# Expert stage of a two-block model: a plain-fp32 gather with the first expert apart, and the order of the last weight loads

## The chip, the cores and the metric

One core of one Trainium2 chip runs the whole program in one launch. The metric is the device time in microseconds (us). Three runs of the kernel before are shown; their median is the number that the change is measured against.

## The reference

The model is two blocks, all in fp32: a hybrid of a state-space mixer, a gated recurrence and a feed-forward layer over 528 tokens, then attention, a second recurrence and an expert layer over 512 tokens. The change touches only the expert layer, which is the last thing before the final normalisation:

```python
def expert_choice_ffn(h, w_router, w_gate, w_up, w_down):
    b, s, d = h.shape                      # 1, 512, 1024
    cap = EC_CAPACITY * s // N_EXPERTS     # 64 tokens for each of 16 experts
    affinity = jax.nn.softmax((h @ w_router).astype(jnp.float32), axis=-1)
    top_val, top_idx = lax.top_k(affinity.transpose(0, 2, 1), cap)
    xe = jax.vmap(lambda hb, ib: hb[ib])(h, top_idx)
    act = jax.nn.silu(jnp.einsum('becd,edf->becf', xe, w_gate)) * jnp.einsum('becd,edf->becf', xe, w_up)
    ye = jnp.einsum('becf,efd->becd', act, w_down) * top_val[..., None].astype(h.dtype)
    return jax.vmap(lambda yb, ib: jnp.zeros((s, d), yb.dtype).at[ib.reshape(-1)].add(yb.reshape(-1, d)))(ye, top_idx)

    # the end of the second block
    x = x + expert_choice_ffn(rms_norm(x, norm_ffn_g[l]), w_router[l], w_exp_gate[l], w_exp_up[l], w_exp_down[l])
    return rms_norm(x, norm_final_g)
```

Each expert picks its 64 tokens of 512. Gate and up weights are 1024 x 2048, down weights 2048 x 1024, so the 16 experts read 403 MB.

## The kernel before, in words

`two_blocks` calls the stages one after the other. The last is `expert_ffn` (names in the trace begin with `moe_`). All engines run their own instruction streams, written out by hand and tied by semaphores.

**Chunks and the ring.** An expert's 2048 hidden columns are cut into 4 chunks of 512, so there are 64 chunks, n = 0 to 63, with e = n // 4 the expert and c = n % 4 its chunk. Each chunk has three weight pieces of 2 MB: part 0 is gate, 1 is up, 2 is down. They pass through `ring`, a buffer of 7 slots. The list `items` gives the order of the loads: gate and up of chunk n, then down of chunk n - 1. The SyncE engine issues one DMA for each item (L3485); from the eighth item on it first waits until the item 7 places back is used: for gate and up that is `hidden_made`, for down it is `out_made`.

**Routing.** TensorE makes the logits (L3494), VectorE the affinities (L3726 to L3733). `turn_tokens` (L3503) transposes the raw rows `xg` to token-major form. ScalarE scales them into `z_high` in fp32r (`split_high`, L3647), and VectorE writes the rest that fp32r cut off into `z_low` (`split_low`, L3740). VectorE finds each expert's 64 largest affinities in 8 rounds of 8 (L3747 and L3748), and in seven of these rounds a `split_low` stands behind the two search instructions. A scan gives each chosen token its place (L3752), and `one_hot(b)` (L3762) makes the selection matrix `hot` for a batch of 4 experts, 256 columns.

**Gather.** `gather(b, v)` (L3532) multiplies token rows by `hot`: 2 blocks of 128 features, 4 blocks of 128 tokens, and two passes (low and high), 16 fp32r matmuls in all with 256 columns each; `take` (L3663) copies the result to `xe`, which lies in `xg`. Batch 0 runs its four gathers before the first chunk; those of batch b + 1 stand one behind the last chunk of each expert of batch b.

**A chunk on TensorE.** `hidden(n, half)` (L3550) is 8 fp32 matmuls of 64 x 512 a half, gate and up in two halves of the array. Between its halves stands `turn(n - 1)` (L3564), the transposes of the activation of the chunk before, which ScalarE copies to `act_t` (L3677). Then comes `output(n - 1)` (L3578), 8 matmuls with down weights. On ScalarE `silu` (L3670) and on VectorE `product` (L3779) make the activation. For each expert, `turn_scatter` (L3589) makes the matrix that puts rows back, and `combine` (L3603), from the chunk after the next expert's first on, multiplies it with `ye` (copied at L3804); VectorE adds to `acc` (L3787). The loop over n has one more pass than chunks, for the last turn and output. Then come the last four combines, the final sums of squares (L3629, L3640), the scale (L3705, L3707), eight scalings (L3811) and eight stores (L3488).

In the profile a plain fp32 matmul stands as two records and an fp32r one as one, each with its own weight load; transposes have one record.

## Time and profile before

| | before |
|---|---|
| runs | 2951.44, 2952.47, 2947.84 us |
| median of the three | 2951.44 us |
| profiled execution, span from first to last instruction | 2951.6 us |
| profiled execution, its own time | given only as that span |
| TensorE matmul busy | 2675.1 us (91%) |
| TensorE weight loads busy | 1940.4 us (66%) |
| VectorE busy | 1261.7 us (43%) |
| ScalarE busy | 800.0 us (27%) |
| mean granted TensorE clock | 0.960 of full |
| largest shares of the chain that ended last | DMA 21%, TensorE 11%, VectorE 1% |
| HBM read, written | 568.84 MB, 38.99 MB |

The span is what one profiled execution took on the core; the runs are separate executions. Busy shares are means over stages with different limits: the expert stage begins at 1967 us and lasts a third of the span. The chain of waits is followed back from the last instruction, at each step to what released it. A granted clock of 1.00 is 2.4 GHz and 0.50 is 1.2 GHz.

### The profile page before, as it was taken

How to read it: one execution, taken by the hardware profiler on the slowest of the kernel's cores; microseconds unless marked ns; L12 is line 12 of the kernel's file. 1: busy time of each engine (PE TensorE's matmuls, PEld its weight loads, DVE VectorE, ACT ScalarE, POOL GpSimd, SP SyncE). 2: the span in 40 equal slices, each digit the busy share in tenths (PEclk: the TensorE clock that was granted, in tenths of full speed). 3: DMA queues.
4: the chain of work that ended last, by engine and by line, in shares of the span. 5: the costliest groups of instructions: out<-in, count | busy, mean ns of one | idle time of the engine just before them, and what ended most of it. 6: DMA issues, size and time to landing. Idle time of an engine off the chain costs nothing. (4 is left out here: it accounts for less than half of the span.)

```text
span 2951.6 us, 44568 instructions
## 1 busy us (share of the span) xinstructions
PE 2675.1 (91%) x18822; PEld 1940.4 (66%) x18822; DVE 1261.7 (43%) x2123; ACT 800.0 (27%) x1304; POOL 112.8 (4%) x90
## 2 busy tenths in 40 slices
PE   8997789799999998999889999879989899989887
PEld 8996677699999998778668888654333333333222
DVE  7764666444566632666363335751111111111112
ACT  3220454432434321543253332531000000000001
POOL 0000021000000000000002221000000000000000
PEclk9998899899999999999989999989999999999999
DMA  5447331455322233334420000548999999999996
GB/s 161 130 129 120 108 123 61 149 164 159 114 90 86 78 123 129 114 129 154 161 77 1 2 1 34 176 179 363 430 430 431 430 431 430 431 431 431 431 430 258
DMA packets 144437, 613.09 MB, mean 208 GB/s; under 512 B 37808, under 2 KB 57392, under 8 KB 119216
## 3 DMA queue, kind: packets, MB, share of 16 engines
q1 hardware_dynamic: 120576, 574.13, 50.7%
q10 hardware_dynamic: 23664, 36.11, 3.5%
q8 instruction: 151, 2.47, 0.3%
q14 instruction: 46, 0.38, 0.0%
HBM read 568.84 MB, written 38.99 MB: 206 GB/s over the span
## 5 line engine op out<-in xcount | busy, mean ns | idle before, releaser
L3550 PE MATMUL moe_bank<-moe_ring,xg 128*64 128x512 f32 x2048 | 494.1, 626 | 90.6 <-DMA moe_ring<-in_w_exp_up 89.3
L3550 PEld LDWEIGHTS moe_bank<-moe_ring,xg 128*64 128x64 f32 x2048 | 156.0, 142 | 370.9 <-issue 362.1
L3779 DVE TENSOR_TENSOR moe_sg<-moe_sg,moe_bank 64x512 f32<-64x512 f32 x64 | 44.1, 690 | 584.7 <-ACT moe_sg L3670 584.7
L3578 PE MATMUL moe_bank<-moe_ring,moe_act_t 128*64 128x512 f32 x1024 | 230.6, 592 | 0.5 <-ACT moe_act_t L3677 0.5
L66 PE MATMUL ffn_prod<-ffn_x_low,ffn_w_high 128*128 128x264 f32 x704 | 200.7, 285 | 5.9 <-PEq L142 5.9
L66 PE MATMUL in_bank<-x_low,in_w_high 128*128 128x264 f32 x640 | 187.3, 293 | 17.9 <-DVE in_w_low L982 9.2
L68 PE MATMUL ffn_prod<-ffn_x_high,ffn_w_high 128*128 128x264 f32 x704 | 200.9, 285 | 0.0
L67 PE MATMUL ffn_prod<-ffn_x_high,ffn_w_low 128*128 128x264 f32 x704 | 199.9, 284 | 0.0
L68 PE MATMUL in_bank<-x_high,in_w_high 128*128 128x264 f32 x640 | 184.6, 288 | 0.0
L67 PE MATMUL in_bank<-x_high,in_w_low 128*128 128x264 f32 x640 | 184.3, 288 | 0.0
L3578 PEld LDWEIGHTS moe_bank<-moe_ring,moe_act_t 128*64 128x64 f32 x1024 | 73.3, 137 | 146.3 <-issue 145.7
L3677 ACT COPY moe_act_t<-moe_bank 128x256 f32<-128x256 f32 x64 | 23.8, 372 | 515.7 <-PE moe_bank L3564 515.7
L66 PE MATMUL front_bank<-front_x_low,front_w_high 128*128 128x512 f32 x368 | 147.9, 402 | 11.8 <-DVE front_w_low L2505 11.7
L3787 DVE TENSOR_TENSOR acc<-acc,moe_bank 128x512 f32<-128x512 f32 x128 | 82.2, 684 | 174.2 <-PE moe_bank L3603 174.2
L67 PE MATMUL front_bank<-front_x_high,front_w_low 128*128 128x512 f32 x368 | 144.3, 392 | 0.0
L68 PE MATMUL front_bank<-front_x_high,front_w_high 128*128 128x512 f32 x368 | 144.1, 392 | 0.0
L66 PEld LDWEIGHTS ffn_prod<-ffn_x_low,ffn_w_high 128*128 128x128 f32 x704 | 133.1, 189 | 6.1 <-issue 6.1
L66 PEld LDWEIGHTS in_bank<-x_low,in_w_high 128*128 128x128 f32 x640 | 123.2, 192 | 19.6 <-issue 9.6
L67 PEld LDWEIGHTS ffn_prod<-ffn_x_high,ffn_w_low 128*128 128x128 f32 x704 | 133.2, 189 | 0.0
L68 PEld LDWEIGHTS ffn_prod<-ffn_x_high,ffn_w_high 128*128 128x128 f32 x704 | 133.0, 189 | 0.0
L67 PEld LDWEIGHTS in_bank<-x_high,in_w_low 128*128 128x128 f32 x640 | 123.8, 193 | 0.4 <-issue 0.2
L68 PEld LDWEIGHTS in_bank<-x_high,in_w_high 128*128 128x128 f32 x640 | 123.5, 193 | 0.0
(549 smaller groups left out, 5696.8 us busy)
## 6 DMA issues: line engine op xcount, KB each, us to landing
moe_ring<-in_w_exp_gate SPq DMA_DIRECT2D x64, 2048.0 KB, 27.7
moe_ring<-in_w_exp_up SPq DMA_DIRECT2D x64, 2048.0 KB, 21.3
moe_ring<-in_w_exp_down SPq DMA_DIRECT2D x64, 2048.0 KB, 25.9
front_w<-in_w_in SPq DMA_DIRECT2D x50, 512.0 KB, 3.6
ffn_w<-in_w_up SPq DMA_DIRECT2D x44, 512.0 KB, 4.4
in_w<-in_w_in SPq DMA_DIRECT2D x40, 512.0 KB, 4.1
ffn_w<-in_w_down SPq DMA_DIRECT2D x16, 704.0 KB, 4.0
p<-front_out ACTq DMA_DIRECT2D x35, 256.0 KB, 2.0
```

The source lines that it names most:

```text
L66: nc.tensor.matmul(to, w_high, x_low, start=start, stop=False)
L67: nc.tensor.matmul(to, w_low, x_high, start=False, stop=False)
L68: return nc.tensor.matmul(to, w_high, x_high, start=False, stop=stop)
L3550: last = nc.tensor.matmul(bank[64 * g:64 * g + 64, s], xe[:, (e // BATCH) % 2, k, at:at + CAPACITY], ring[:, slot_of(n, g), k * HALF:(k + ...
L3578: last = nc.tensor.matmul(bank[64 * h:64 * h + 64, 3 + e % 2], act_t[:, s, j], ring[:, slot, at:at + HALF], start=(c == 0 and j == 0), sto ...
L3677: nc.scalar.copy(act_t[:, s].rearrange("p j n -> p (j n)"), bank[:, 2, s * FT * CAPACITY:(s + 1) * FT * CAPACITY]).then_inc(act_t_ready, 1)
L3779: nc.vector.tensor_tensor(sg[0:CAPACITY, s], sg[0:CAPACITY, s], bank[64:64 + CAPACITY, s], ALU.mult).then_inc(act_ready, 1)
L3787: nc.vector.tensor_tensor(acc[:, FT * h + q], acc[:, FT * h + q], bank[:, part_bank(e, q) + h], ALU.add).then_inc(part_added, 1)
```

## The change

It has three parts.

1. `z_tok` and `hot` are plain fp32. There is no `z_low`: ScalarE's copies (`take_tokens`) are the whole of the token rows, the eight `split_low` on VectorE are gone, and a gather has one matmul in fp32 where it had two in fp32r.
2. Batch 0 is gathered in parts. `gather_first` gathers the first expert alone before the first chunk, with 32 matmuls of 64 columns into bank 4, and `take_first` copies them. The other three experts follow in four gathers of 8 matmuls with 192 columns, one behind each chunk of expert 0, through banks 5 and 6. `hidden` waits for the first copy at n = 0 and for all of batch 0 at n = 4. Batches 1 to 3 keep their places, with 8 matmuls of 256 columns.
3. The last seven items are gate and up of chunks 62 and 63 and then down of 61, 62 and 63. TensorE's last steps are written out in that order.

```diff
-        z_tok = sb("z_tok", [P, 2, TT, D_MODEL], F32R)
-        z_high, z_low = z_tok[:, 0], z_tok[:, 1]
-        hot_r = sb("hot", [P, 2, TT, BATCH, CAPACITY], F32R)
-        hot = hot_r[:].bitcast(F32)
+        z_tok = sb("z_tok", [P, TT, D_MODEL])
+        hot = sb("hot", [P, 2, TT, BATCH, CAPACITY])
...
-        for n in range(CHUNKS_ALL + 1):
-            if n < CHUNKS_ALL:
-                items += [(n, 0), (n, 1)]
+        for n in range(LAST):
+            items += [(n, 0), (n, 1)]
             if n >= 1:
                 items += [(n - 1, 2)]
+        items += [(n, part) for n in (LAST, LAST + 1) for part in range(2)] + [(n, 2) for n in (LAST - 1, LAST, LAST + 1)]
...
+                def gather_first():
+                    pe.wait_ge(hot_ready, 1)
+                    for k in range(KT):
+                        for t in range(TT):
+                            last = nc.tensor.matmul(bank[:, 4, k * CAPACITY:(k + 1) * CAPACITY], z_tok[:, t, k * P:(k + 1) * P],
+                                                    hot[:, 0, t, 0], start=(t == 0), stop=(t == TT - 1))
+                    last.then_inc(xe_made, 1)
+
                 def gather(b, v):
-                    to = 4 + v if b == 0 else 7
-                    if v == 0:
+                    if b == 0:
+                        to, first = 5 + v % 2, 1
+                        if v >= 2:
+                            pe.wait_ge(xe_ready, v)
+                    else:
+                        to, first = 7, 0
                         pe.wait_ge(hot_ready, b + 1)
-                    if b >= 1:
                         pe.wait_ge(scatter_ready, BATCH * (b - 1) + v + 1)
+                    width = (BATCH - first) * CAPACITY
                     for j in range(2):
                         k = 2 * v + j
                         for t in range(TT):
-                            for part in (z_low, z_high):
-                                last = nc.tensor.matmul(bank[:, to, j * WIDE:(j + 1) * WIDE], part[:, t, k * P:(k + 1) * P],
-                                                        hot_r[:, b % 2, t].rearrange("p e s -> p (e s)"),
-                                                        start=(t == 0 and part is z_low),
-                                                        stop=(t == TT - 1 and part is z_high))
+                            last = nc.tensor.matmul(bank[:, to, j * width:(j + 1) * width], z_tok[:, t, k * P:(k + 1) * P],
+                                                    hot[:, b % 2, t, first:].rearrange("p e s -> p (e s)"),
+                                                    start=(t == 0), stop=(t == TT - 1))
...
-                for v in range(BATCH):
-                    gather(0, v)
-                pe.wait_ge(xe_ready, BATCH)
-                for n in range(CHUNKS_ALL + 1):
+                gather_first()
+                for n in range(LAST + 1):
                     e, c = n // FC, n % FC
-                    if n < CHUNKS_ALL:
-                        hidden(n, 0)
+                    hidden(n, 0)
                     if n >= 1:
                         turn(n - 1)
-                    if n < CHUNKS_ALL:
-                        hidden(n, 1)
-                    if n >= 1:
+                    hidden(n, 1)
+                    if 1 <= n < LAST:
                         output(n - 1)
-                    if n < CHUNKS_ALL and c == 2:
+                    if e == 0:
+                        gather(0, c)
+                    if c == 2:
                         turn_scatter(e)
-                    if n < CHUNKS_ALL and c == 3 and e // BATCH + 1 < BATCHES:
+                    if c == 3 and e // BATCH + 1 < BATCHES:
                         gather(e // BATCH + 1, e % BATCH)
                     if n >= FC + 1:
                         combine((n - FC - 1) // FC, (n - FC - 1) % FC)
+                for half in range(2):
+                    hidden(LAST + 1, half)
+                combine(EXPERTS - 2, FC - 2)
+                output(LAST - 1)
+                turn(LAST)
+                output(LAST)
+                combine(EXPERTS - 2, FC - 1)
+                turn(LAST + 1)
+                output(LAST + 1)
...
                 for r in range(CAPACITY // 8):
                     step(nc.vector.max(best[:], left))
                     step(nc.vector.match_replace(left, best[:], left, -1.0))
-                    if r >= 1:
-                        split_low(r)
```

The order on TensorE from the last place transposes to the end of chunk 1, before (`moe_hot` by `moe_z_tok` is a gather, `moe_ring` by `xg` is hidden, `moe_ring` by `moe_act_t` is output):

```order
L3517 MATMUL moe_bank<-ident,moe_sg 128x16 x4
L3532 MATMUL moe_bank<-moe_hot,moe_z_tok 128x256 x64
L3550 MATMUL moe_bank<-moe_ring,xg 64x512 x24
L3564 MATMUL moe_bank<-ident,moe_sg 128x64 x4
L3550 MATMUL moe_bank<-moe_ring,xg 64x512 x8
L3578 MATMUL moe_bank<-moe_ring,moe_act_t 64x512 x8
```

The same place now:

```order
L3519 MATMUL moe_bank<-ident,moe_sg 128x16 x4
L3528 MATMUL moe_bank<-moe_hot,moe_z_tok 128x64 x32
L3564 MATMUL moe_bank<-moe_ring,xg 64x512 x16
L3545 MATMUL moe_bank<-moe_hot,moe_z_tok 128x192 x8
L3564 MATMUL moe_bank<-moe_ring,xg 64x512 x8
L3578 MATMUL moe_bank<-ident,moe_sg 128x64 x4
L3564 MATMUL moe_bank<-moe_ring,xg 64x512 x8
L3592 MATMUL moe_bank<-moe_ring,moe_act_t 64x512 x8
L3545 MATMUL moe_bank<-moe_hot,moe_z_tok 128x192 x8
```

The 64 wide gather matmuls became 32 narrow ones; hidden(0) is now followed by a gather, and hidden(1) with its turn and output(0) by the next.

The order on TensorE at the end, from hidden(62) on, before:

```order
L3550 MATMUL moe_bank<-moe_ring,xg 64x512 x8
L3578 MATMUL moe_bank<-moe_ring,moe_act_t 64x512 x8
L3589 MATMUL moe_bank<-ident,moe_hot_aff 128x128 x4
L3603 MATMUL moe_bank<-moe_scatter,moe_ye 128x512 x2
L3550 MATMUL moe_bank<-moe_ring,xg 64x512 x8
L3564 MATMUL moe_bank<-ident,moe_sg 128x64 x4
L3550 MATMUL moe_bank<-moe_ring,xg 64x512 x8
L3578 MATMUL moe_bank<-moe_ring,moe_act_t 64x512 x8
L3603 MATMUL moe_bank<-moe_scatter,moe_ye 128x512 x2
L3564 MATMUL moe_bank<-ident,moe_sg 128x64 x4
L3578 MATMUL moe_bank<-moe_ring,moe_act_t 64x512 x8
L3603 MATMUL moe_bank<-moe_scatter,moe_ye 128x512 x8
```

The same place now, from the second half of hidden(62):

```order
L3564 MATMUL moe_bank<-moe_ring,xg 64x512 x8
L3603 MATMUL moe_bank<-ident,moe_hot_aff 128x128 x4
L3617 MATMUL moe_bank<-moe_scatter,moe_ye 128x512 x2
L3564 MATMUL moe_bank<-moe_ring,xg 64x512 x16
L3617 MATMUL moe_bank<-moe_scatter,moe_ye 128x512 x2
L3592 MATMUL moe_bank<-moe_ring,moe_act_t 64x512 x8
L3578 MATMUL moe_bank<-ident,moe_sg 128x64 x4
L3592 MATMUL moe_bank<-moe_ring,moe_act_t 64x512 x8
L3617 MATMUL moe_bank<-moe_scatter,moe_ye 128x512 x2
L3578 MATMUL moe_bank<-ident,moe_sg 128x64 x4
L3592 MATMUL moe_bank<-moe_ring,moe_act_t 64x512 x8
L3617 MATMUL moe_bank<-moe_scatter,moe_ye 128x512 x6
```

The output of chunk 61 moved behind hidden(63), turn(62) moved out of hidden(63) to stand right before its output, and the last combine of expert 14 stands ahead of the last turn instead of behind the last output.

## Rows read from the trace of the kernel before

**Rows 1.** Chain of waits: start us, us, engine, what, at the stage's middle and end.

```profile
2588.57 3.65 PE moe_bank L3550 x16
...
2617.71 3.65 PE moe_bank L3550 x16
...
2910.97 3.65 PE moe_bank L3550 x16
...
2918.60 3.43 PE moe_bank L3578 x16
2922.03 1.06 PE moe_bank L3603 x4
2923.79 3.65 PE moe_bank L3578 x16
2927.44 1.08 PE moe_bank L3603 x4
```

**Rows 2.** Windows: length, busy us of each engine, granted clock, DMA share, GB/s.

```profile
2004.00:2013.00 9.00, 8.28 (x44) 3.92 (x44) 0.00 (x0) 1.89 (x3) 0.00 (x0) 1.00 0.00 0
2013.50:2014.00 0.50, 0.50 (x4) 0.17 (x2) 0.40 (x1) 0.07 (x1) 0.00 (x0) 1.00 0.96 197
```

**Rows 3.** Timeline from the search to the second release of the ring: start us, us.

```profile
1973.74 0.68 DVE L3747 MAX8 moe_best<-moe_sg 16x8 f32<-16x512 f32 x1
...
1975.23 0.68 DVE L3747 MAX8 moe_best<-moe_sg 16x8 f32<-16x512 f32 x1
...
1977.40 0.67 DVE L3747 MAX8 moe_best<-moe_sg 16x8 f32<-16x512 f32 x1
...
1993.69 1.22 DVE L3762 TENSOR_TENSOR moe_hot<-slots,moe_place_tok 128x1024 fp32r<-128x1024 f32 x1
...
1995.06 10.07 PE L3532 MATMUL moe_bank<-moe_hot,moe_z_tok 128*128 128x256 f32 x64 [1.74 <-DVE moe_hot L3762]
...
2005.85 10.52 PE L3550 MATMUL moe_bank<-moe_ring,xg 128*64 128x512 f32 x48 [0.72 <-ACT xg L3663]
...
2012.97 0.33 SPq L3485 DMA_DIRECT2D moe_ring<-in_w_exp_down  x1
...
2020.38 0.33 SPq L3485 DMA_DIRECT2D moe_ring<-in_w_exp_up  x1
```

**Rows 4.** Windows at two changes of the granted clock.

```profile
1969.00:1970.00 1.00, 1.00 (x8) 1.00 (x7) 0.00 (x0) 0.98 (x2) 0.00 (x0) 0.64 0.54 229
1995.00:2000.00 5.00, 4.94 (x23) 4.97 (x24) 0.64 (x1) 0.59 (x1) 0.00 (x0) 0.50 1.04 441
2000.00:2003.00 3.00, 3.00 (x27) 3.00 (x27) 0.00 (x0) 0.59 (x1) 0.00 (x0) 1.00 0.96 410
```

**Rows 5.** Timeline, 128x128 fp32 weights at half and full clock, and under one column.

```profile
1545.39 0.55 PEld L2942 LDWEIGHTS rw_bank<-rw_sm,rw_a_first 128*128 128x128 f32 x2
1545.82 0.55 PEld L2943 LDWEIGHTS rw_bank<-rw_z,rw_sm 128*128 128x128 f32 x2
...
1805.23 0.30 PEld L2942 LDWEIGHTS rw_bank<-rw_sm,rw_a_first 128*128 128x128 f32 x2
1805.45 0.30 PEld L2943 LDWEIGHTS rw_bank<-rw_z,rw_sm 128*128 128x128 f32 x2
...
1965.64 1.05 PE L3274 MATMUL merge_bank<-merge_one,merge_sq_sum 128*128 128x1 f32 x8
```

**Rows 6.** Timeline near the end: a half-clock group, the last turn, the waiting add.

```profile
2896.38 5.35 PE L3550 MATMUL moe_bank<-moe_ring,xg 128*64 128x512 f32 x16 [2.49 <-DMA moe_ring<-in_w_exp_up]
...
2922.92 0.40 PE L3564 MATMUL moe_bank<-ident,moe_sg 64*128 64x64 f32 x4
...
2928.55 1.28 DVE L3787 TENSOR_TENSOR acc<-acc,moe_bank 128x512 f32<-128x512 f32 x2 [0.37 <-PE moe_bank L3603]
```

**Rows 7.** Timeline, a gather of batch 1 between chunks.

```profile
2046.12 2.18 PE L3532 MATMUL moe_bank<-moe_hot,moe_z_tok 128*128 128x256 f32 x16
```

**Rows 8.** Line L3485, the ring's loads from issue to landing.

```profile
DMA to landing us min/median/max: 7.6/25.8/34.4
```

More of the change, by code:

```diff
@@ L3386, in expert_ffn @@
     CHUNKS_ALL = EXPERTS * FC
+    LAST = CHUNKS_ALL - 2
     WIDE = BATCH * CAPACITY
@@ L3428, in expert_ffn @@
         z_turned = sem("z_turned")
-        z_high_ready = sem("z_high_ready")
         z_tok_ready = sem("z_tok_ready")
@@ L3452, in expert_ffn, with gathers_through @@
         stored = sem("stored")
+        def gathers_through(b):
+            return 1 + BATCH * (b + 1)
         def part_bank(e, q):
@@ L3540, in hidden @@
                     if half == 0:
-                        if n % (BATCH * FC) == 0:
-                            pe.wait_ge(xe_ready, BATCH * (e // BATCH + 1))
+                        if n == 0:
+                            pe.wait_ge(xe_ready, 1)
+                        elif n == FC or n % (BATCH * FC) == 0:
+                            pe.wait_ge(xe_ready, gathers_through(e // BATCH))
                         if n >= 2:
@@ L3654, in _ @@
                 act.wait_ge(scale_ready, 1)
-                split_high(0)
+                take_tokens(0)
                 act.wait_ge(route, MOE_LOGITS)
@@ L3658, in _, with take_first @@
                 for n in range(1, 2 * TT):
-                    split_high(n)
+                    take_tokens(n)
+                def take_first():
+                    act.wait_ge(xe_made, 1)
+                    nc.scalar.copy(xe[:, 0, :, 0:CAPACITY], bank[:, 4].rearrange("p (k n) -> p k n", k=KT)).then_inc(xe_ready, 1)
                 def take(b, v):
-                    act.wait_ge(xe_made, BATCH * b + v + 1)
-                    nc.scalar.copy(xe[:, b % 2, 2 * v:2 * v + 2], bank[:, 4 + v if b == 0 else 7].rearrange(
+                    to, first = (5 + v % 2, CAPACITY) if b == 0 else (7, 0)
+                    act.wait_ge(xe_made, gathers_through(b - 1) + v + 1)
+                    nc.scalar.copy(xe[:, b % 2, 2 * v:2 * v + 2, first:], bank[:, to, 0:2 * (WIDE - first)].rearrange(
                         "p (k n) -> p k n", k=2)).then_inc(xe_ready, 1)
@@ L3684, in turned_scatter @@
                     nc.scalar.copy(scatter[:, e % 2], bank[:, 7]).then_inc(scatter_ready, 1)
-                for v in range(BATCH):
-                    take(0, v)
+                take_first()
                 for n in range(CHUNKS_ALL + 1):
@@ L3693, in _ @@
                         silu(n)
+                    if e == 0:
+                        take(0, c)
                     if n < CHUNKS_ALL and c == 2:
@@ L3759, in one_hot @@
                     if b >= 2:
-                        dve.wait_ge(xe_made, BATCH * (b - 1))
+                        dve.wait_ge(xe_made, gathers_through(b - 2))
                     grid = [P, TT, BATCH, CAPACITY]
-                    nc.vector.tensor_tensor(hot_r[:, b % 2], slots[:].unsqueeze(1).unsqueeze(1).broadcast_to(grid),
+                    nc.vector.tensor_tensor(hot[:, b % 2], slots[:].unsqueeze(1).unsqueeze(1).broadcast_to(grid),
                                             place_tok[:, :, BATCH * b:BATCH * b + BATCH].unsqueeze(3).broadcast_to(grid),
```

15 lines of the change are left out of this document (4 added, 11 removed).

## The prediction

> **What bounds the kernel now.** I read the chain of waits first. From the middle of the expert stage to its end it alternates between TensorE and the ring load of an up weight: chunk after chunk TensorE finishes early and waits for DMA. Equal places in it lie 29.14 us apart for two chunks, 2588.57 and 2617.71 [rows 1], so a chunk of three 2 MB loads takes 14.57 us and one load 4.86 us. The end of the kernel is therefore the start of an unbroken run of loads, plus 4.86 us each, plus a tail after the last.
>
> Then the windows around the start of the stage. The ring takes seven loads, and the eighth waits for the first chunk's hidden matmuls. Between 2004 and 2013 us the DMA engines carry nothing (share 0.00); from 2013.5 on they are busy [rows 2]. So the start of the first expert is the one place where an earlier TensorE brings the whole train of 185 remaining loads forward, one for one. The instruction that decides it is the SyncE issue at 2012.97 [rows 3].
>
> At the end, the chain leaves DMA at 2910.97, when the last up weights have landed. Two down pieces follow, so the last load lands about 2 x 4.86 later, at L = 2920.7. The last output matmuls start at 2923.79 and end at 2927.44 [rows 1], 6.7 us after L: the end is held by TensorE's work, not by the last transfer alone. Everything behind 2927.44 (24.2 us to the end of the 2951.6 us span) is the same in both kernels but for one add.
>
> **Term 1, the places chain on VectorE.** A round of the top-64 search without the split takes 1.49 us (1973.74 to 1975.23), one with it 2.17 us (1975.23 to 1977.40) [rows 3]. The eight splits go; the first lay beside other work, seven lay in rounds: 7 x 0.66 = 4.6 us. The one-hot at 1993.69 starts and the gather at 1995.06 [rows 3] moves to 1990.4. The ScalarE copies stay where they are and are done long before.
>
> **Term 2, the first gather.** Before: 64 matmuls of 256 columns in fp32r, one record each, 10.07 us [rows 3], the first 4.9 us at a granted clock of 0.50 (1.2 GHz), the rest at 1.00 (2.4 GHz) [rows 4]. Now: 32 matmuls with 64 columns in plain fp32. Plain fp32 matmuls show as two records each, so 64 records again, and each carries a 128x128 weight load. In the stage before, such weight loads come in pairs 0.43 us apart at half clock (1545.39, 1545.82) and 0.22 us apart at full clock (1805.23, 1805.45), so 0.215 and 0.11 us a record; eight records with a single column take 1.05 us, again 0.11 apart [rows 5]. A narrow matmul thus costs its weight load: four times fewer columns save nothing. 64 records cost 13.8 us at half clock, 7.0 us at full clock, 9.5 us if the clock rises 4.9 us in as before (23 records at 0.215, 41 at 0.11).
>
> Which? The clock fell to 0.5 inside 1969 to 1970 although TensorE ran without a break (PE 1.00, PEld 1.00): what it had just run were narrow matmuls, 1 column [rows 5], then transposes [rows 4]. It rose at 2000 after five microseconds of 256-column matmuls. The new gather is of the narrow kind, so I take half clock for the whole of it: 1990.4 + 13.8, plus 0.2 for the last record, is 2004.4. The evacuation stays 0.7 us (2005.13 to 2005.85) [rows 3], so hidden(0) starts at 2005.1 instead of 2005.85: 0.75 us gained.
>
> But hidden(0) then begins at half clock, and before it ran at full clock. A group of 16 that began just before a half-clock stretch took 5.35 instead of 3.65 us [rows 6]. I estimate that the clock rises 4.6 us into hidden(0), about as long as the 4.9 us after 1995.06; this loses half of that, 2.3 us (bounds 0 and 7.1, the whole of hidden(0), which took 7.1 from 2005.85 to 2012.97 [rows 3]). Term 2 with term 1: the eighth load is issued 2.3 - 0.75 = **1.55 us later** than before (bounds -7 and +6.4).
>
> The Trainium skill, page "TensorE: Matmul & The Clock Gate", section "LDWEIGHTS (loading the stationary operand)", prices a weight load at its columns over 1.2 GHz whatever the clock. By it, an estimate, 64 loads of 128 columns would be 6.8 us even at half clock. The pairs at half clock contradict it, with 0.215 us a record.
>
> **Term 3, feeding the ring in the first expert.** The other three experts of the batch are now gathered between the chunks, four times 8 matmuls of 192 columns: 16 records. The 128-column records of rows 5 cost 0.11 us at full clock; in proportion 192 columns are 0.16 and 256 columns 0.21, so 2.6 us a gather. Batches 1 to 3 gather 256 columns: 16 x 0.21 = 3.4 us instead of 2.1 (2.18 us with the last one's drain) [rows 7]; the 1.3 us more, twelve times, lie in the TensorE idle time of a chunk: 14.57 less 7.4 + 3.4 + 1.1 = 2.7 us, and slots are freed several loads ahead. If that cover failed it would cost 12 x 1.3 = 16 us, but landings take 25.8 us from issue at the median [rows 8], five loads ahead.
>
> Right after T, the end of hidden(0), there is no such lead. Two loads go out at T; the next two after a gather and hidden(1) with its turn, 2.6 + 7.4 = 10.0 us on (7.4 from the issue at 2012.97 to that at 2020.38 [rows 3]). The shortest landing is 7.6 us after issue [rows 8], so the third lands at T + 17.6 instead of T + 7.6 + 2 x 4.86 = T + 17.3: 0.3 us lost. Adding output 3.4, gather 2.6 and hidden 7.4 a chunk, 0.6 for turning the scatter and 3.4 for the batch-1 gather, hidden(4) ends at T + 54.2; the 12th load lands at T + 61.8 instead of 61.4: 0.4 more. **Sum 0.7 us** (bounds 0, and 3 if each gather takes 0.5 us longer). From then on TensorE needs 12 us a chunk against 14.57.
>
> **Term 4, the end.** The last up weights now land three loads before the last, at L - 14.6. From there TensorE owes hidden(63) 7.1, combine 1.06, output(61) 3.4 (2918.60 to 2922.03), turn and its copy 0.87 (2922.92 [rows 6] to 2923.79), output(62) 3.4, combine 1.06, turn 0.87, output(63) 3.65 = 21.4 us: L + 6.8 [rows 1]. Before it was L + 6.7. The loads were permuted, and the work behind them with them. The add that waited 0.37 us for its combine after the last output [rows 6] is already made: -0.35. Against that, the slack before hidden(63) shrinks from 2.0 us to 0.6 (hidden(62) at L - 24.3, then 7.4, 0.5 to 0.6 for the scatter turn and 1.1; before, output(61) lay there too, and the next load was 4.86 us further off), so the 1.7 us half-clock loss of rows 6, which was hidden, would show with 1.1; I take half of it. **Sum +0.2 us** (bounds -3.3, the last output waiting for its load alone, and +1.5).
>
> **Sum.** 1.55 + 0.7 + 0.2 = +2.5 us. The span of 2951.6 becomes 2954.1; the median of the three runs, 2951.44, is 0.2 below the span, so **2953.9 us**. That is 0.08%; a measurement of this kernel can tell about 0.2%, 5.9 us, from no change.
>
> **Rivals.** (a) *The clock rises during the gather as before.* Gather 9.5 us, hidden(0) at full clock from 2000.8: 5.05 us earlier; with terms 3 and 4 -4.1 us, **2947.3**. For it: it rose 4.9 us into the old gather, and TensorE has no gaps now either. Against it: the fall at 1969.3 under narrow matmuls.
> (b) *Weight loads do not slow with the clock.* 64 x 0.11 = 7.0 us: hidden(0) at 1998.3, 7.5 us earlier, less 2.3 for its own half clock; with 3 and 4 -4.3 us, **2947.1**, and up to 2945 if the clock rises sooner. Against it: the half-clock pairs of rows 5. That is also what the page's rule would give here.
> (c) *The end loses its TensorE queue*: output(63) waits only for its load: 3.3 us less in term 4 instead of +0.2, **2950.4**. Against it: the 21.4 us counted above.
> (d) *Slower: the clock stays low through all of hidden(0).* 7.1 us instead of 2.3, the ring then fed late with 2.7 instead of 0.7, and the 1.1 us at the end in full: 4.8 + 2.0 + 0.6 more, **2961.3**. It decides once the SyncE issue comes more than about 5 us later than 2012.97. For it: TensorE pauses 0.7 us between gather and hidden(0). Against it: wide matmuls raised the clock within 5 us.
> (e) *The change does not do what it says*, DMA still stopping for as long, is near my forecast: the stop gets longer, not shorter.
>
> **Chances.** Forecast 0.60; (a) 0.18; (b) 0.07; (c) 0.05; (d) 0.10. The forecast's own range is 2951 to 2957.5, from the bounds of terms 2 to 4. The whole range reaches to (a) and (b) below and part of the way to (d): 2946 to 2958. Faster than 2945.5: the lower edges of (a) and (b), 0.10. Slower than 2957.3: (d) and the upper edge of the forecast, 0.16. Within 0.2%: 0.74.
>
> **What would show it.** The one-hot at about 1989, the gather at 1990.4 and 13 to 14 us long with a granted clock of 0.50 all through; the SyncE issue of the eighth load at about 2014.5; gathers of 2.6 us between the first chunks; hardly any DMA pause after 2016; the last output matmuls ending about 6.8 us after the last landing. The forecast is wrong if the gather runs at 1.00 after some microseconds or its records come 0.11 us apart at half clock, if loads pause again in the first expert, or if the last output starts on its load.

## The result, and the profile after

The kernel with the change took 2956.32 us (median of 17 runs, 2953.18 to 2962.97), the kernel before 2951.17 us (17 runs, 2945.82 to 2955.27): a ratio of the means of 1.0021 with a 95% interval of 1.0015 to 1.0027. It is slower by 4.4 to 8.0 us: clear of no change, but only 0.2%. Measured again beside the last experiments it was 2956.53 against 2952.01, 1.0017 (1.0008 to 1.0026). The medians lie 5.15 us apart, and 4.5 us the second time; the forecast was 2953.9 us, 2.5 us above before, with a range of 2946 to 2958.

The page of the profiled execution (its own time 2954.39 us):

```profile
span 2952.5 us, 44691 instructions
...
PE 2698.3 (91%) x18886; PEld 1959.4 (66%) x18886; DVE 1256.3 (43%) x2115; ACT 799.4 (27%) x1305; POOL 112.6 (4%) x90
...
DMA 18%; PE 14%; DVE 1%; ACT 0%; issue 0%; DVEq 0%; ACTq 0%
...
L3564 PE MATMUL moe_bank<-moe_ring,xg 128*64 128x512 f32 x2048 | 486.7, 619 | 72.3 <-DMA moe_ring<-in_w_exp_up 71.7
```

The hidden matmuls (now L3564) still wait for up weights and for little else. What changed lies at the two ends of that train of loads. Its start, as the timeline of the kernel after (start us, us, engine, line):

```profile
1970.47 0.68 DVE L3767 MAX8 moe_best<-moe_sg 16x8 f32<-16x512 f32 x1
...
1971.96 0.68 DVE L3767 MAX8 moe_best<-moe_sg 16x8 f32<-16x512 f32 x1
...
1985.80 1.22 DVE L3780 TENSOR_TENSOR moe_hot<-slots,moe_place_tok 128x1024 f32<-128x1024 f32 x1
...
1987.17 13.89 PE L3528 MATMUL moe_bank<-moe_hot,moe_z_tok 128*128 128x64 f32 x64 [1.74 <-DVE moe_hot L3780]
...
2001.73 9.07 PE L3564 MATMUL moe_bank<-moe_ring,xg 128*64 128x512 f32 x32 [0.68 <-ACT xg L3685]
...
2010.84 0.33 SPq L3487 DMA_DIRECT2D moe_ring<-in_w_exp_down  x1
...
2021.20 0.33 SPq L3487 DMA_DIRECT2D moe_ring<-in_w_exp_up  x1
...
2024.52 2.87 PE L3545 MATMUL moe_bank<-moe_hot,moe_z_tok 128*128 128x192 f32 x16
```

And its windows (length, busy us of the engines, granted clock, DMA share, GB/s):

```profile
1976.00:1977.00 1.00, 0.00 (x0) 0.00 (x0) 0.96 (x2) 0.00 (x0) 0.00 (x0) 0.50 0.88 377
1988.00:2000.00 12.00, 12.00 (x59) 12.00 (x58) 0.00 (x0) 0.00 (x0) 0.00 (x0) 0.50 1.01 429
2001.50:2005.50 4.00, 3.77 (x10) 1.23 (x12) 0.00 (x0) 1.46 (x2) 0.00 (x0) 0.50 0.00 0
2006.00:2010.00 4.00, 4.00 (x22) 1.32 (x20) 0.00 (x0) 0.00 (x0) 0.00 (x0) 1.00 0.00 0
...
2930.00:2934.00 4.00, 4.00 (x12) 1.40 (x12) 2.26 (x4) 1.42 (x3) 0.00 (x0) 0.60 0.00 0
```

Against [rows 3]: every search round is 1.49 us, and the gather takes 13.89 us in place of 10.07. TensorE was busy for all of 1988 to 2000, yet the granted clock was 0.50 (1.2 GHz), and it stayed there through the first 4 us of hidden(0); before, it rose in the gather [rows 4].

In this execution the stages ahead, which are the same code, were 3 us shorter (in the 13 profiles the expert stage begins anywhere from 1963.4 to 1970.8 us), so all that follows counts from the stage's first ring load (1967.16 before, 1964.23 after). "Eighth issue" is the SyncE issue that hidden(0) releases (2012.97 in [rows 3], 2010.84 here); the column "hidden(0)" runs from its first matmul to that issue. A load lands with the last of its 16 completions; "last landing" is that of the 192nd weight load, 2920.52 before and 2920.69 after. All pieces are in us, from one profiled execution each, so a whole stage can lie some 3 us off what the medians say; the experiments are already in the table.

| kernel | first load to gather | gather | hidden(0) | first load to eighth issue | eighth issue to last landing | last landing to end | whole stage |
|---|---|---|---|---|---|---|---|
| before | 27.90 | 10.07 | 7.12 | 45.81 | 907.55 | 31.09 | 984.45 |
| the change | 22.94 | 13.89 | 9.11 | 46.61 | 909.85 | 31.82 | 988.28 |
| the change, again | 22.94 | 13.89 | 9.08 | 46.58 | 910.32 | 31.86 | 988.76 |
| only the end of the change | 27.48 | 9.61 | 7.12 | 44.93 | 907.69 | 32.85 | 985.47 |
| only plain fp32 | 22.94 | 16.56 | 7.11 | 47.34 | 907.85 | 31.12 | 986.31 |
| change, old end | 22.94 | 13.89 | 9.17 | 46.68 | 911.08 | 31.11 | 988.87 |
| two experts first | 23.55 | 9.33 | 7.12 | 40.72 | 909.70 | 30.91 | 981.33 |
| 128 columns, 64 used | 23.35 | 10.25 | 7.13 | 41.41 | 912.20 | 33.03 | 986.64 |
| unused wide matmuls | 22.78 | 7.25 | 7.12 | 37.83 | 910.63 | 31.86 | 980.32 |
| late gathers | 23.37 | 13.89 | 9.44 | 47.37 | 910.30 | 31.84 | 989.51 |
| two experts, late | 23.42 | 9.46 | 7.12 | 40.72 | 907.48 | 30.85 | 979.05 |
| two experts, late, again | 22.94 | 10.10 | 7.11 | 40.87 | 907.65 | 30.96 | 979.48 |
| the same with unused matmuls | 22.94 | 8.98 | 7.12 | 39.76 | 907.72 | 33.03 | 980.51 |

The change loses 3.8 us in the stage (4.3 the second time): 0.8 before the eighth issue, 2.3 (2.8) between it and the last landing, and 0.7 (0.8) behind that. The medians are 1.3 us (0.2 us) further apart than that; no piece accounts for it.

The end, timeline of the kernel after:

```profile
2906.25 7.09 PE L3564 MATMUL moe_bank<-moe_ring,xg 128*64 128x512 f32 x32 [0.41 <-DMA moe_ring<-in_w_exp_up]
...
2924.24 3.65 PE L3592 MATMUL moe_bank<-moe_ring,moe_act_t 128*64 128x512 f32 x16 [0.46 <-ACT moe_act_t L3704]
2929.97 4.56 PE L3617 MATMUL moe_bank<-moe_scatter,moe_ye 64*128 64x512 f32 x12 [2.08 <-DVE acc L3805]
```

The last output ends 7.2 us after the last landing (6.9 before, [rows 1]). TensorE then stands idle for 2.08 us until the combines of the last expert. In the kernel before, a combine lay there first and only 1.48 us were idle:

```profile
2929.98 1.99 PE L3603 MATMUL moe_bank<-moe_scatter,moe_ye 64*128 64x512 f32 x8 [1.48 <-DVE acc L3787]
```

And the combines after the change run into a stretch at half clock: the clock was 0.60 on average over 2930 to 2934.

### The profile page after: what moved, and what is told of

Its sections match the earlier page's. It is cut to its first block and busy times, and to the rows that moved or that the text cites. A ratio compares the mean times of both kernels' runs of the same rounds, so it can differ in the third digit from the quotient of the medians.

```text
span 2952.5 us, 44691 instructions
## 1 busy us (share of the span) xinstructions
PE 2698.3 (91%) x18886; PEld 1959.4 (66%) x18886; DVE 1256.3 (43%) x2115; ACT 799.4 (27%) x1305; POOL 112.6 (4%) x90
## 5 line engine op out<-in xcount | busy, mean ns | idle before, releaser
L3564 PE MATMUL moe_bank<-moe_ring,xg 128*64 128x512 f32 x2048 | 486.7, 619 | 72.3 <-DMA moe_ring<-in_w_exp_up 71.7
L3564 PEld LDWEIGHTS moe_bank<-moe_ring,xg 128*64 128x64 f32 x2048 | 149.8, 141 | 351.2 <-issue 342.7
L66 PEld LDWEIGHTS in_bank<-x_low,in_w_high 128*128 128x128 f32 x640 | 123.0, 192 | 19.1 <-issue 10.3
```

The costliest lines, as they stand in the source:

```text
L66: nc.tensor.matmul(to, w_high, x_low, start=start, stop=False)
L3564: last = nc.tensor.matmul(bank[64 * g:64 * g + 64, s], xe[:, (e // BATCH) % 2, k, at:at + CAPACITY], ring[:, slot_of(n, g), k * HALF:(k + ...
```

## The experiments

### The parts by themselves

Four kernels shared the runs of before (2952.60 us, 33 runs). First, the kernel before with the third part of the change alone, the order of the last loads and of TensorE's last steps:

```diff
-        for n in range(CHUNKS_ALL + 1):
+        for n in range(LAST):
...
+        items += [(n, part) for n in (LAST, LAST + 1) for part in range(2)] + [(n, 2) for n in (LAST - 1, LAST, LAST + 1)]
...
```

> The kernel before with part 3 alone (order of the last seven loads and of TensorE's last steps). Theory (the loads are permuted and TensorE's work with them): from the last weight landing to the end of the last output 7 us as before, and the granted clock may fall once in the last combines; 0 to +1 us against before. Rival (the new order is worth something: the last output waits for its load alone): -3 us. Rival (the tail costs most of the change's +5 us): +3 us or more.

Measured: 2952.41 us (11 runs), 1.0003 (0.9995 to 1.0012). The order of the end is worth nothing that can be told. The table has 1.8 us more behind the last landing. Two falls of the clock are in it: one slowed the first half of hidden(62), which took 5.35 us instead of 3.65, so that hidden(63) started 1.08 us after its up weights had landed instead of 0.14, and one slowed the last combines.

Second, the kernel before with plain fp32 alone, all four experts gathered first:

```diff
-                            for part in (z_low, z_high):
-                                last = nc.tensor.matmul(bank[:, to, j * WIDE:(j + 1) * WIDE], part[:, t, k * P:(k + 1) * P],
-                                                        hot_r[:, b % 2, t].rearrange("p e s -> p (e s)"),
+                            last = nc.tensor.matmul(bank[:, to, j * WIDE:(j + 1) * WIDE], z_tok[:, t, k * P:(k + 1) * P],
+                                                    hot[:, b % 2, t].rearrange("p e s -> p (e s)"),
...
-                    if r >= 1:
-                        split_low(r)
```

> The kernel before with part 1 alone: plain fp32, all four experts of batch 0 gathered before the first chunk. Theory: search chain 4.6 us shorter; gather of 64 records with 256 columns, 0.43 us each at half clock for some 5 us, then 0.21: about 16 us instead of 10.1; hidden(0) at full clock, 7.1 us, since these are wide matmuls; the eighth load leaves 1.4 us later than before, no feeding loss: +1 to +2 us against before. Rival (plain fp32 as such costs the change's time, batches 1 to 3 too): +5 us.

Measured: 2952.76 us (11 runs), 1.0003 (0.9994 to 1.0012). Its timeline:

```profile
1986.30 16.56 PE L3528 MATMUL moe_bank<-moe_hot,moe_z_tok 128*128 128x256 f32 x64 [1.74 <-DVE moe_hot L3747]
...
2043.86 3.72 PE L3528 MATMUL moe_bank<-moe_hot,moe_z_tok 128*128 128x256 f32 x16
```

and its windows:

```profile
1986.30:1991.30 5.00, 5.00 (x12) 4.02 (x13) 0.58 (x1) 0.00 (x0) 0.00 (x0) 0.50 1.01 433
1991.40:2002.80 11.40, 11.40 (x53) 9.74 (x52) 0.00 (x0) 1.76 (x3) 0.00 (x0) 1.00 0.69 295
```

The stretch to the gather is 5.0 us shorter and the gather 6.5 us longer. But this gather, wide and otherwise placed like the change's, saw the clock rise 5 us in, and hidden(0) ran at full clock. The stretch from the eighth issue to the last landing is within 0.3 us that of before. The stage of this profile is 1.9 us longer than before, which the medians do not show.

Third, the change with the old end:

```diff
-        for n in range(LAST):
+        for n in range(CHUNKS_ALL + 1):
...
-                for half in range(2):
-                    hidden(LAST + 1, half)
...
```

> The change with part 3 undone. Theory: the end costs 0.7 us of the change's 5, so -0.7 us against the change, +3 to +5 against before; start of the stage as in the change (gather 13.9 us at 0.50, hidden(0) 9.1 us). Rival (the tail costs most): back to before, 0.

Measured: 2955.63 us (11 runs), 1.0014 (1.0005 to 1.0023). The loss is there without the third part, and it is not there with plain fp32 alone. What costs is thus the second part, the first expert alone with the rest of its batch between the chunks: 2.9 us between these two medians, and in the table 2.6 us of stage.

Fourth, the change with the first **two** experts in the first gather (128 columns) and the other two between the chunks:

```diff
-                            last = nc.tensor.matmul(bank[:, 4, k * CAPACITY:(k + 1) * CAPACITY], z_tok[:, t, k * P:(k + 1) * P],
-                                                    hot[:, 0, t, 0], start=(t == 0), stop=(t == TT - 1))
+                            last = nc.tensor.matmul(bank[:, 4 + k // 4, k % 4 * P:(k % 4 + 1) * P], z_tok[:, t, k * P:(k + 1) * P],
+                                                    hot[:, 0, t, 0:2].rearrange("p e s -> p (e s)"), start=(t == 0), stop=(t == TT - 1))
...
-                        to, first = 5 + v % 2, 1
+                        to, first = 5 + v % 2, 2
...
```

ScalarE's copy is made in two halves, the first beside the second half of the gather, and `hidden` waits for the whole batch at n = 8 instead of 4.

> The change with the first TWO experts in the first gather: the same 32 matmuls and 64 weight loads, 128 columns instead of 64, the other two gathered between the chunks with 128 columns instead of 192. Theory (narrow matmuls do not raise the clock, and a matmul costs its weight load whether it has 64 or 128 columns): the granted clock rises inside the gather, which takes 9 to 11 us instead of 13.9, hidden(0) 7.1 instead of 9.1, gathers between chunks 1.9 instead of 2.9: the eighth load leaves about 5.5 us earlier than in the change, total -6 to -8 us against the change, -1 to -3 against before. Rival (the clock rises only by time, or weight loads keep it down): gather 13.9 and hidden(0) 9.1 as in the change, total +0.6 for the longer copy. Rival (columns cost): gather 15 us or more.

Measured: 2948.57 us (11 runs), 0.9990 (0.9981 to 0.9999), 7 us less than the third kernel. Its timeline:

```profile
1988.24 9.33 PE L3530 MATMUL moe_bank<-moe_hot,moe_z_tok 128*128 128x128 f32 x64 [1.74 <-DVE moe_hot L3787]
1998.29 7.09 PE L3569 MATMUL moe_bank<-moe_ring,xg 128*64 128x512 f32 x32 [0.72 <-issue]
```

and its windows:

```profile
1988.30:1992.30 4.00, 4.00 (x19) 4.00 (x20) 0.52 (x1) 0.00 (x0) 0.00 (x0) 0.50 1.03 442
1992.40:1997.40 5.00, 5.00 (x47) 4.98 (x45) 0.00 (x0) 0.58 (x1) 0.00 (x0) 1.00 1.00 426
```

Twice the columns take 4.6 us less. A record comes every 0.21 us at half clock (19 in 4 us) and every 0.11 us at full clock (47 in 5 us), as with 64 columns (13.89 / 64 = 0.217 us at half clock). The difference of the two gathers is thus the clock, which rose 4.1 us in.

### Is it the width of what TensorE streams?

The two-expert kernel also has less to gather later, so the next four kernels (before beside them: 2952.18 us, 35 runs) separate the two. First the change with a first gather that streams 128 columns and throws the second 64 away; nothing else is gathered earlier:

```diff
-                            last = nc.tensor.matmul(bank[:, 4, k * CAPACITY:(k + 1) * CAPACITY], z_tok[:, t, k * P:(k + 1) * P],
-                                                    hot[:, 0, t, 0], start=(t == 0), stop=(t == TT - 1))
+                            last = nc.tensor.matmul(bank[:, 4 + k // 4, k % 4 * P:(k % 4 + 1) * P], z_tok[:, t, k * P:(k + 1) * P],
+                                                    hot[:, 0, t, 0:2].rearrange("p e s -> p (e s)"), start=(t == 0), stop=(t == TT - 1))
...
-                    nc.scalar.copy(xe[:, 0, :, 0:CAPACITY], bank[:, 4].rearrange("p (k n) -> p k n", k=KT)).then_inc(xe_ready, 1)
+                    nc.scalar.copy(xe[:, 0, :, 0:CAPACITY],
+                                   bank[:, 4:6].rearrange("p b (k n) -> p (b k) n", n=P)[:, :, 0:CAPACITY]).then_inc(xe_ready, 1)
```

> The change, but the first gather streams 128 columns per matmul and throws the second 64 away: the same 64 records with the same weight loads, and only what TensorE streams is doubled. Theory (a narrow stream of 64 columns keeps the granted clock at 0.50): the clock rises some 5 us into the gather as with the two-expert gather, the gather takes 9.3 us in place of 13.9, hidden(0) 7.1 in place of 9.1, the eighth load is issued 40.5 us after the stage's first in place of 46.6, and the kernel takes 6 us less than the change, about 2949 to 2950. Rival (the clock stayed low by chance, or for the place of the gather in time): gather 13.9 us, about 2956. Second rival (the two-expert kernel gained by having one gather fewer to make later): clock as in the theory, but the end no earlier than 2953.

Measured: 2951.02 us (11 runs), 0.9992 (0.9984 to 1.0001). Its windows:

```profile
1990.00:1995.00 5.00, 5.00 (x26) 5.00 (x25) 0.00 (x0) 0.00 (x0) 0.00 (x0) 0.51 1.03 439
1995.00:2000.00 5.00, 4.33 (x39) 4.13 (x40) 0.00 (x0) 0.81 (x2) 0.00 (x0) 1.00 1.00 423
```

The clock rose 6.0 us into the gather, which took 10.25 us, hidden(0) was at full clock, and the eighth issue came 5.2 us sooner than in the change. Streaming columns that nobody reads makes the change some 5 us faster (2956.3 and 2956.5 us in its own measurements; the kernel with late gathers, which gathers narrowly and was measured beside this one, took 2955.72). The theory holds for the clock. The profiled execution does not show the whole gain: its own time was 2954.05 us, with a fourth stretched load (the last section tells of them) and two falls of the clock near the end. The second rival falls by its number, since the median lies below 2953, but there is something in it: the two-expert kernel stood 4.0 us below the before of its own runs and this one 1.2 us, so having less to gather later seems to be worth some 3 us as well.

Then the change with unused matmuls of 512 columns ahead of the gather:

```diff
+                for _ in range(12):
+                    nc.tensor.matmul(bank[:, 6], ident[:], xg[:, 0], start=True, stop=True)
                 pe.wait_ge(route, MOE_PLACES)
...
                 def gather_first():
+                    for _ in range(2):
+                        nc.tensor.matmul(bank[:, 6], ident[:], xg[:, 0], start=True, stop=True)
                     pe.wait_ge(hot_ready, 1)
```

> The change, with 12 unused matmuls of 512 columns while TensorE waits for the search, and 2 before it waits for the one-hot rows (nothing reads their result). Theory (the gather ran at half clock because of what TensorE did ahead of it and in it): the clock is at 1.00 when the gather starts; if the 64-column stream can keep it, the gather takes 7.2 us and hidden(0) 7.1, the eighth load is issued 38 us after the first, about 2948; if the narrow stream itself lets the clock fall again, it falls within the gather, which then takes 9 to 12 us and hidden(0) up to 9.1: 2951 to 2954. Rival (the clock has no part): the gather takes 13.9 us and the time is that of the change, about 2956, or up to 1 us more for the matmuls that end late.

Measured: 2950.61 us (12 runs), 1.0003 (0.9990 to 1.0017), in two groups: eight runs at 2946.6 to 2951.0, four at 2960.2 to 2963.1. The profiled execution is one of the eight. Its timeline:

```profile
1989.37 1.98 PE L3528 MATMUL moe_bank<-xg,ident 128*128 128x512 f32 x4
1991.19 7.25 PE L3532 MATMUL moe_bank<-moe_hot,moe_z_tok 128*128 128x64 f32 x64
1999.12 7.09 PE L3568 MATMUL moe_bank<-moe_ring,xg 128*64 128x512 f32 x32 [0.68 <-ACT xg L3689]
```

The granted clock was 1.00 before, in and after the gather: the same 64 narrow records take 7.25 us, 0.113 each, about half of 0.217, and the eighth issue comes 8.8 us sooner than in the change. These narrow matmuls did not lower a clock that was up, in 7.25 us; they did not raise one that was down, in 13.9 us. The group at 2960 was not profiled. The mean granted clock of its four executions, 0.963 against 0.966 to 0.970 in the other eight, speaks for executions in which the unused matmuls did not get the clock up and only delayed the gather; that is argued, not shown.

### Where the 2.3 us behind the eighth issue come from

For this, landings were compared one by one. The third kernel of these four: the change with the later gathers after chunks 2, 3, 4 and 4 in place of 1 to 4:

```diff
-                    if e == 0:
-                        gather(0, c)
+                    if e == 0 and c >= 1:
+                        gather(0, c - 1)
+                    if n == 3:
+                        gather(0, 3)
```

> The change, with the four gathers of the rest of the batch after the second, third and fourth chunk (1, 1, 2) in place of one after each. Theory (the 2.87 us of gather ahead of the second release, where the ring has just been idle, is what stretches the stretch from the first release to the last landing from 907.6 to 910 us): the landing interval of 8.05 us goes back to 5.6, the stretch to 907.6 to 908.2, clock and gather unchanged (13.9 us), so 2 us less than the change: about 2954. Rival (what stretches it is the sum of the gathers or the load hiccups): the stretch stays at 910 or more, as the gap only moves to the fourth chunk, and the time stays at 2956.

Measured: 2955.72 us (11 runs), 1.0013 (1.0004 to 1.0021). The rival was right. As a rule a load lands 4.85 us after the one before it. In the change the tenth load lands 8.05 us after the ninth (2023.44 to 2031.49; 5.56 in the kernel before) and the nineteenth 5.99 after the eighteenth (4.85 before); here it is 5.45 and 7.74. The first gap went, as expected, and the second grew by 1.75 us, because now three gathers stand in a row on TensorE, two of 192 columns and the first of batch 1 with 256:

```profile
2023.66 2.87 PE L3545 MATMUL moe_bank<-moe_hot,moe_z_tok 128*128 128x192 f32 x16
2037.45 2.87 PE L3545 MATMUL moe_bank<-moe_hot,moe_z_tok 128*128 128x192 f32 x16
2051.67 8.92 PE L3545 MATMUL moe_bank<-moe_hot,moe_z_tok 128*128 128x192 f32 x48
```

Fourth kernel: the two-expert gather and the late gathers together.

```diff
-                        to, first = 5 + v % 2, 1
+                        to, first = 5 + v % 2, 2
...
-                    if e == 0:
-                        gather(0, c)
+                    if e == 0 and c >= 1:
+                        gather(0, c - 1)
+                    if n == 3:
+                        gather(0, 3)
...
```

> Both together: the first two experts in the first gather (128 columns) and the four later gathers put late. Theory: eighth load 40.7 us after the first, and 907.6 to 908.2 us from there to the last landing: 2 us less than the two-expert kernel, about 2946.5, and 6 us less than before. Rival (the later gathers only move the gap): 2948.5, as the two-expert kernel.

Measured: 2947.34 us (11 runs), 0.9979 (0.9970 to 0.9987). Its timeline on SyncE, the first two releases:

```profile
2008.14 0.33 SPq L3489 DMA_DIRECT2D moe_ring<-in_w_exp_down  x1
2008.51 0.43 SPq L3489 DMA_DIRECT2D moe_ring<-in_w_exp_gate  x1
2015.56 0.33 SPq L3489 DMA_DIRECT2D moe_ring<-in_w_exp_up  x1
```

and on TensorE, the gathers behind chunk 4:

```profile
2045.26 7.29 PE L3549 MATMUL moe_bank<-moe_hot,moe_z_tok 128*128 128x128 f32 x48
```

The second release comes 7.4 us after the first, as in [rows 3], in place of 10.4. The tenth load lands 5.72 us after the ninth, the nineteenth 4.85 after the eighteenth, and the stretch is 907.48 us, that of before. Lateness at either place costs, and in these profiles only a kernel that is late at neither has the old figure: 907.5 to 907.9 for before, the end alone, plain fp32 alone and the kernels of this form, 909.7 to 912.2 for the six executions with a gather ahead of the second release and 910.3 for the one with three gathers, 8.92 us of them, behind chunk 4. How much of a single figure is the gathers and how much the stretched loads of the last section differs from profile to profile.

### Again, side by side

Measured side by side (before 2952.01 us, 27 runs): the change, the best kernel, and that kernel with 8 unused matmuls before the wait for the search (the edit as above, with 8 in place of 12 and none in `gather_first`).

> The change itself, beside the other kernels of this call. Expected as first measured: 1.002 of before, about 2956, the clock at 0.50 through the whole first gather (13.9 us), hidden(0) 9.1 us, the eighth load issued 46.6 us after the first, and 909.8 us from there to the last landing.

Measured: 2956.53 us (11 runs), 1.0017 (1.0008 to 1.0026). The eighth issue is 46.58 us after the first load, the rest as expected within 0.6 us.

> The two-expert gather with late gathers a second time, to have it beside the change and before on one chip: 0.998 of before, about 2947, with the eighth load issued 40.7 us after the first and 907.5 us from there to the last landing. If the first measurement was luck, the interval takes in 1.

Measured: 2947.15 us (11 runs), 0.9983 (0.9974 to 0.9992), 9.4 us less than the change. Measured twice, it is 0.2% faster than before; here it is 0.3% faster than the change.

> The two-expert gather with late gathers, plus 8 unused matmuls of 512 columns while TensorE waits for the search (nothing reads their result). Theory: where they bring the clock to 1.00 before the gather, it takes 7.2 us in place of 9.4, the eighth load comes 2.2 us earlier and the kernel takes about 2945.5; where they don't, they cost nothing, as they end before the search does, and the time is 2947.3. Rival: as with the 12 matmuls on the change, the runs fall into two groups, and the higher one lies 10 us or more above, so that the median is no better than 2947.3.

Measured: 2947.09 us (11 runs), 0.9984 (0.9975 to 0.9993): no better, though in one group. In the profiled execution the clock had fallen again at 1985.46, 3.5 us before the gather, and rose 3.3 us into it; the gather took 8.98 us. The eighth issue was still 1.1 us earlier, and two falls of the clock near the end, where the stage lost 2 us behind the last landing, took it back in this execution.

## Why the prediction was right, and where it was not

The time lay in the range and on the forecast's side. But the change cost 5.15 us by the medians (4.5 the second time), where +2.5 was forecast. The mechanism at the start was the one named, and the experiments bear it out; that is not luck. Three sizes were off, and in part they cancel: in the profile the terms came to 0.80 + 2.30 + 0.73 = 3.8 us, against 1.55 + 0.7 + 0.2.

One thing in the sum did no harm but did not compare like with like: 2951.44 us is the time of a run and 2951.6 us a span. In every run with both numbers the time is 1.8 to 2.0 us above the span, so the profiled execution before took about 2953.5 us (an estimate from these), 2 us above the median.

**Term 1** (4.6 us from the search): the eight rounds went from 16.56 to 11.93 us, 4.63. Right.

**Term 2** (eighth load 1.55 us later): 0.80 us later. The gather was forecast at 13.8 us and the last record's drain, all at half clock; it took 13.89 us at 0.50. The choice of half clock rested on one row, the fall of the clock at 1969 under narrow matmuls [rows 4], and the experiments bear it out. With 64 columns the clock stayed at 0.50 in all four profiles with this gather where nothing raised it ahead, and with 128 or 256 columns in plain fp32 it rose 3.3 to 6.0 us in, in all six. The rest is hidden(0), forecast at 2.3 us more and measured at 1.99: the clock rose 4.0 us into it and not 4.6. The front of the stage gave 0.33 more than the search did. There the clock rose at 1968.22, 4 us after the first load; in the five profiles with plain fp32 in which the clock rose 3.9 to 4.7 us after the first load the stretch to the gather is 22.94 us, and in the four in which it rose 7.2 to 8.9 us after it 23.35 to 23.55.

**Rival (b)**, weight loads that do not slow with the clock, is out: 64 records took 13.89 us at 1.2 GHz and 7.25 us at 2.4 GHz. The price that the Trainium skill gives in "TensorE: Matmul & The Clock Gate", section "LDWEIGHTS (loading the stationary operand)", is the same at either clock, 0.107 us for 128 columns (an estimate by its formula). It comes near the 0.113 us a record at full clock and does not hold at half clock, where a record takes 0.217 us. **Rival (a)**, the clock rises in the gather, is false for this kernel and is what the 128-column gathers did. In the Trainium skill, same page, section "What's actually happening", the clock is set by how busy TensorE has been. The row 1988 to 2000 has it busy for 12.00 of 12.00 us with no rise, so busy time as the profile counts it did not decide it here.

**Term 3** (0.7 us for feeding the ring, bounds 0 and 3): 2.3 and 2.8 us in the two profiles. This is the step that was most wrong in size. And 2.3 flatters it: counted from T, the eighth issue, the nineteenth load lands 3.4 us later than before (65.54 us against 62.13), 2.8 us in the second profile, and after that load the rest of the first profile is 1.1 us shorter because one of the stretched loads told of below lost 0.3 us in place of 1.4. Two numbers in the term were wrong. The small one: a 192-column record took 0.179 us (2.87 / 16), not 0.16, so a gather takes 2.87 us and not 2.6. The large one: "The shortest landing is 7.6 us after issue, so the third lands at T + 17.6". Its landing came 10.3 us after its issue and 20.65 us after T. The row was read for a transfer that it doesn't describe. The 7.6 us belong to the eighth load, issued when nothing was in flight; the tenth is issued while the ninth still runs. In the kernel before, the tenth was issued 7.4 us after T and landed 18.3 us after it, where T + 7.6 + 2 x 4.86 gives 17.3: the check was in the trace and would have shown that the sum was short. Against that, the tenth landed 2.3 us later than before, and not 0.3. Nineteen loads in, the second late place cost 1.14 us (5.99 against 4.85), forecast at 0.4; this landing came 65.5 us after T and not 61.8. The cover for the wider gathers of batches 1 to 3 (3.72 us each, forecast 3.4) held: behind the nineteenth load the landings come 4.85 us apart as before, but for the stretched ones told of below. At the median a load of the ring still lands 24.6 us, five loads, after its issue (line L3487, against [rows 8]):

```profile
DMA to landing us min/median/max: 7.7/24.6/34.9
```

**Term 4** (+0.2 us, bounds -3.3 and +1.5): +0.73 and +0.77 us. By the ends of the output, 0.28 us later, and the add already made, 0.46 us sooner, it would be -0.18 us, and the three executions with this end and no fall of the clock in it do have 30.85 to 30.96 us against 31.09 to 31.12. The 1.1 us of a late hidden(63), of which half was put in, did not occur in this profile. It did in three of the ten profiles with the new end (only the end, 128 columns with 64 used, and the last with unused matmuls): their last landing to end is 32.85 to 33.03 us. What came in its place was not thought of: taking the combine away from behind the last output leaves TensorE idle for 2.08 us there, and in 7 of the 10 profiles with the new end the clock was at 0.50 for 3.4 us in the combines that follow (0.9 us lost), in none of 3 with the old. Medians cannot show it. That the idle time is the cause is argued, not shown: in the other three the same 2.08 us were idle and the clock stayed up.

**Rival (c)** is out, the last output stood behind TensorE's queue, 3.55 us after the last landing. **Rival (d)**, slower at 2961.3, didn't occur: hidden(0) got its clock back after 4.0 us. **Rival (e)** can't be told from the forecast by its time. The stop between the seventh landing and the eighth issue was 8.63 us (2002.21 to 2010.84, with a DMA share of 0.00 in 2006 to 2010) against 8.52 before, so it did not get shorter. So the forecast stood, but 2.7 us for late feeding were set down in (d) alone, and they belonged in the forecast.

## What to carry to other kernels

Making a first piece narrower saves nothing where each matmul costs its weight load (64 and 128 columns both 0.21 to 0.22 us a record at half clock here), and it can cost the clock: read the granted clock of the narrow stretch, not only whether TensorE is busy. Widening that piece to 128 columns took about 5 us off here, even with columns that nobody reads.

Where a ring has been idle, the second release counts as much as the first: compare when the loads after a restart land with when they were issued, load by load, before pricing anything put between two releases. Here, work moved off the start cost nothing only where slots were freed several loads ahead.

## What the runs showed that was not expected

**A 2 MB load lands with its slowest part.** Each load has 16 completions in the trace. Those of the ninth load of the change lie 0.94 us apart from first to last, those of the tenth 3.30, while the windows show little idle time on average (DMA share, kernel after):

```profile
2018.00:2023.00 5.00, 5.00 (x26) 1.70 (x24) 0.69 (x1) 0.59 (x1) 0.00 (x0) 1.00 1.04 400
2023.00:2024.00 1.00, 1.00 (x8) 0.29 (x4) 0.00 (x0) 0.00 (x0) 0.00 (x0) 1.00 0.68 229
2024.00:2025.00 1.00, 1.00 (x7) 0.48 (x4) 0.00 (x0) 0.00 (x0) 0.00 (x0) 1.00 1.02 410
2025.00:2026.00 1.00, 1.00 (x8) 1.00 (x7) 0.00 (x0) 0.00 (x0) 0.00 (x0) 1.00 0.84 344
```

A gap of half a microsecond on average stands beside a landing that is 3.2 us late. Of the tenth load eleven completions come within 0.6 us of its first, and the last one comes 1.3 us after the fifteenth: the mean share hides what looks like a few late engines, one above all. The Trainium skill, page "DMA: Bandwidth & Descriptors", section "Why a DMA increments its semaphore by 16 and not by 1", says that each engine that works on a transfer posts a count of its own; the 16 completions of each load agree. Why a few lose so much more when the second release is late stays open.

**Every 235 to 250 us a landing comes 5.9 to 6.6 us after the one before it instead of 4.85**, in all 13 profiles: at 2270.96, 2505.78 and 2745.44 us before, at 2491.45 and 2731.11 after. In these five the time from first to last completion grows by 1.4 to 1.5 us. After the change the one before them, at 2261.49, came after only 5.18 us; in five of the other profiles smaller ones (5.2 to 5.7 us) stand between them. The queue of instructions moves a 16 KB packet about every 30 us, taking 0.9 us; the page of the profile counts 151 of them:

```profile
q8 instruction: 151, 2.47, 0.3%
```

One began 2.5 us before each of the three late landings in the kernel before (2268.49, 2503.30, 2742.98), and 2.5 us before the first and 6.1 us before the second of the two after (2488.98, 2725.01). About one in eight such packets goes with a late load. That they fall in turn on different engines, and cost time where they meet the one that is already last, would fit this; it is a guess, since the packets' records do not name an engine, and it wasn't tried. In the kernel before the three cost 4.3 us of the stage, about as much as the change moved.
